# Two output projections computed as seven products of halves, with the sums of weights made on the chip

## The reference, cut to what matters

```python
mix = jnp.concatenate([y_a, y_b], axis=-1) @ w_out      # (2048 x 1024) @ (1024 x 1024), first block
x = layer_norm(alpha * x + mix, ln_g[layer], ln_b[layer])
...
y = jnp.concatenate([a, r], axis=-1) @ w_out[l]         # second block, same sizes
h = layer_norm_2(DN_ALPHA * h + y, ln_g[l], ln_b[l])
```

## Time and profile before

| | us |
|---|---|
| median of three runs | 3617.89 (3614.83 to 3624.52) |
| the profiled execution | 3618.56 |
| its span, first to last instruction | 3616.7 |

### The profile page before, as it was taken

How to read it: one execution, slowest core, us unless ns; L and a number is a source line. 1 busy time by engine, 2 the same in 40 slices (tenths; PEclk the granted TensorE clock), 3 DMA queues, 4 the chain that set the end, 5 groups by cost and what they waited for, 6 DMA issues and landing times.

```text
span 3616.7 us, 46252 instructions
## 1 busy us (share of the span) xinstructions
PE 3399.0 (94%) x17264; PEld 1815.3 (50%) x17264; DVE 1933.8 (53%) x4680; ACT 1347.7 (37%) x2565; POOL 549.5 (15%) x1001
## 2 busy tenths in 40 slices
PE   8999999999999999999989999999998898998887
PEld 3444544554455445545564455654555643455563
DVE  4326622753274337334562577816768616878742
ACT  2212211222131213123241465514775514786451
POOL 0000021002100110011120201201451111352000
PEclk9999999999999999989989999999999999998998
DMA  5230023002300210141103121021110031110011
GB/s 188 76 99 13 7 76 122 2 19 76 111 1 28 93 62 1 44 154 64 59 26 103 59 76 33 25 99 64 60 49 1 25 113 53 55 51 1 1 37 57
DMA packets 72095, 206.30 MB, mean 57 GB/s; under 512 B 6425, under 2 KB 8001, under 8 KB 71617
## 3 DMA queue, kind: packets, MB, share of 16 engines
q1 hardware_dynamic: 63536, 187.61, 15.4%
q10 hardware_dynamic: 8336, 15.74, 1.2%
HBM read 185.75 MB, written 17.58 MB: 56 GB/s over the span
## 4 chain that ended last, share of the span: by engine, by line
PE 78%; DVE 10%; ACT 6%; issue 5%; POOL 1%; DMA 1%; SPq 0%; ACTq 0%; DVEq 0%; POOLq 0%
PE bank L1989 42%; PE o_acc L2122 6%; PE bank L2105 6%; PE bank L2353 3%; PE bank L2112 3%; PE bank L2240 3%; PE bank L2272 2%; PE bank L2365 2%; PE o_acc L2379 2%; ACT prob_t L1194 1%; PE bank L2202 1%; DVE tmp L1692 1%; PE bank L2033 1%; PE bank L2039 1%; ACT index L1337 1%
## 5 line engine op out<-in xcount | busy, mean ns | idle before, releaser
L1989 PE MATMUL bank<-group_even,weights 128*128 128x512 f32 x1344 | 590.5, 597 | 11.4 <-DMA group_even<-in_x_t 5.9
L1989 PE MATMUL bank<-group_odd,weights 128*128 128x512 f32 x1344 | 591.8, 597 | 6.3 <-ACT tmp L1180 6.2
L1989 PE MATMUL bank<-y_all,weights 128*128 128x512 f32 x1024 | 441.2, 593 | 6.3 <-DVE y_all L1948 6.3
L1989 PEld LDWEIGHTS bank<-group_even,weights 128*128 128x128 f32 x1344 | 254.7, 192 | 322.6 <-issue 321.7
L1989 PEld LDWEIGHTS bank<-group_odd,weights 128*128 128x128 f32 x1344 | 254.8, 192 | 318.8 <-issue 318.3
L1139 ACT ACTIVATE probs<-probs,stat 128x512 f32<-128x512 f32 x256 | 181.7, 711 | 422.2 <-DVE stat L1456 422.2
L1989 PEld LDWEIGHTS bank<-y_all,weights 128*128 128x128 f32 x1024 | 194.2, 190 | 250.3 <-issue 243.0
L2122 PEld LDWEIGHTS o_acc<-lat,val 128*128 128x128 f32 x2048 | 238.8, 195 | 44.2 <-issue 40.2
L2122 PE MATMUL o_acc<-lat,val 128*128 128x128 f32 x2048 | 248.3, 280 | 7.7 <-DVE lat L1521 7.6
L2105 PE MATMUL bank<-k_nope,q_nope 128*32 128x512 f32 x2048 | 233.0, 595 | 0.0
L1507 DVE CUSTOM_DVE_ANT_0 probs<-bank,mask 128x512 f32<-128x512 f32 x256 | 161.4, 687 | 100.9 <-PE bank L2112 100.9
(11 more groups left out here) (396 smaller groups left out, 5151.0 us busy)
## 6 DMA issues: line engine op xcount, KB each, us to landing
weights<-in_w_in SPq DMA_DIRECT2D x101, 512.0 KB, 3.5
weights<-in_w_in_q SPq DMA_DIRECT2D x64, 512.0 KB, 3.4
weights<-in_w_out SPq DMA_DIRECT2D x64, 512.0 KB, 3.5
weights<-in_w_i SPq DMA_DIRECT2D x20, 512.0 KB, 3.4
group_odd<-in_x_t SPq DMA_DIRECT2D x8, 1024.0 KB, 9.1
group_even<-x_t SPq DMA_DIRECT2D x8, 1024.0 KB, 8.0
group_odd<-x_t SPq DMA_DIRECT2D x8, 1024.0 KB, 7.6
weights<-in_w_in_kv SPq DMA_DIRECT2D x12, 512.0 KB, 7.7
```

What stands on the lines that cost most here:

```text
L1989: ins = M(bank(*name)[:], ring[n % SLOTS][:, k * P:(k + 1) * P], rhs[:, k, :], start=(at == 0), stop=(at == chunks - 1))
```

## The change

In `1out` and `2out` the inputs are halved (chunks 0 to 3 of y, from the attention, and 4 to 7) and the 512 tokens too (EARLY and LATE, 256 each). For each pair of output chunks c, d there are seven products of 4 chunks x 256 tokens, where the two tiles of 8 chunks x 512 tokens amount to eight of that size. Four of the seven take sums of weights (t1 to t4) and four take sums of y (s1 to s4).

```diff
+OPENED_BY = {1: 1, 2: 1, 5: 5, 3: 5, 6: 6, 7: 6, 4: 6}
+def product_order(pairs):
+    out = [(0, 1)]
+    for n in range(pairs):
+        out += [(n, 6), (n, 5), (n, 7)]
+        out += [(n + 1, 1), (n, 4), (n, 2), (n, 3)] if n + 1 < pairs else [(n, 2), (n, 4), (n, 3)]
+    return out
```

```diff
+            def project_out(tag, g):
+                for at, (pair, m) in enumerate(product_order(OUT_PAIRS)):
+                    n = WSLOT[(tag + "out", g, at // 2)]
+                    if at % 2 == 0:
+                        pe.wait_ge(w_here[n % SLOTS], W_COUNT[n])
+                    if pair == 0 and m in (6, 5, 7):
+                        pe.wait_ge(y_summed, 3 * stage + {7: 1, 5: 2, 6: 3}[m])
+                    elif pair == 0 and m == 4:
+                        pe.wait_ge(made, BG * g + 2)
+                    elif pair == 0 and m == 2:
+                        pe.wait_ge(made, BG * (g + 1))
+                    elif pair == 0 and m == 3:
+                        pe.wait_ge(y_summed_late, stage + 1)
+                    claim(*name)
+                    for k in range(4):
+                        ins = M(bank(*name)[:, 0:HALF], ring[n % SLOTS][:, at % 2 * TB + k * P:at % 2 * TB + (k + 1) * P], of[:, k, :],
+                                start=(OPENED_BY[m] == m and k == 0), stop=(k == 3), skip_group_check=True)
```

```diff
+            for n, m in product_order(OUT_PAIRS):
+                if m == 1:
+                    V.scalar_tensor_tensor(out=d2, in0=d2, scalar=ALPHA, in1=got.unsqueeze(1).broadcast_to([P, 2, HALF]), ...)
+                    drains(V.scalar_tensor_tensor(out=c[:, EARLY], in0=c[:, EARLY], scalar=ALPHA, in1=got, ...), *name)
+                elif m == 2:
+                    drains(V.scalar_tensor_tensor(out=c[:, LATE], ...), *name)
+                else:
+                    to = d[:, LATE] if m in (6, 3) else d[:, EARLY] if m in (5, 7) else c[:, EARLY]
+                    drains(V.tensor_tensor(to, to, got, ALU.add), *name)
```

```diff
+            def store_pair(n):
+                act.wait_ge(pair_summed, n + 1)
+                act.dma_start(w_sums[n], pair_sums[n % 2]).then_inc(pair_stored[n % 2], 16)
+                if n + 2 < len(SUM_PAIRS):
+                    stage_pair(n + 2)
+            def store_next(g, third):
+                n = 3 * (g - 1) + third
+                if g > 0 and n < len(SUM_PAIRS):
+                    store_pair(n)
@@ ACT, first pass
                 root(("kv_sq", g), KVR, 0, (k_normed, g) if g else None)
+                if g == 0:
+                    stage_pair(0)
+                    stage_pair(1)
+                store_next(g, 0)
                 rope_tables(g)
+                store_next(g, 1)
...
                     drains(A_(val[:, BG * g + b, :], bank("v", g, b)[:], ACT.Copy), "v", g, b)
+                store_next(g, 2)
```

More of the change, by code:

```diff
@@ L409, with is_product, banks_of_tiles @@
 assert len(T) == len(TILES)
+def is_product(name):
+    return name[0] in ("1out", "2out")
+def banks_of_tiles():
+    bank, turn, used, opened = {}, {}, [0] * RING, 0
+    for name in TILES:
+        if is_product(name) and OPENED_BY[name[-1]] != name[-1]:
+            bank[name] = bank[(*name[:-1], OPENED_BY[name[-1]])]
+        else:
+            bank[name] = opened % RING
+            opened += 1
+        turn[name] = used[bank[name]]
+        used[bank[name]] += 1
+    return bank, turn
+BANK, TURN = banks_of_tiles()
 def weight_of(name):
@@ L441, in stream_of @@
 def stream_of(tiles):
-    out = []
+    out, products = [], []
     for name in tiles:
+        if is_product(name):
+            products.append((name, weights_of_product("w_out" if name[0] == "1out" else "w_out2", *name[2:])))
+            if len(products) == 2:
+                number = product_order(OUT_PAIRS).index(name[2:]) // 2
+                out.append(((*name[:2], number), None, [source for _, source in products], name))
+                products = []
+            continue
         if weight_of(name):
@@ L975, in _ @@
             pool.wait_ge(const_made, 4)
+            sum_weights()
             for g in range(G):
@@ L1982, in project @@
                 claim(*name)
-                order = list(range(chunks)) if heads_made is None else [4, 5, 6, 7, 0, 1, 2, 3]
-                for at, k in enumerate(order):
+                for k in range(chunks):
                     if parts and k % 2 == 0:
                         pe.wait_ge(x_part[k // 2], 16)
-                    if heads_made is not None and k == 0:
-                        pe.wait_ge(y1_made, heads_made)
                     ins = M(bank(*name)[:], ring[n % SLOTS][:, k * P:(k + 1) * P], rhs[:, k, :],
-                            start=(at == 0), stop=(at == chunks - 1))
+                            start=(k == 0), stop=(k == chunks - 1))
@@ L2139, in _ @@
                     wait_drained(pe, "mix", g, j)
-                for c in range(KC):
-                    project(("1out", g, c), y_of(g), KC, BG * (g + 1) if c == 0 else None)
+                project_out("1", g)
             second_begins(pe)
```

203 lines of the change are left out of this document (155 added, 48 removed).

## The result

| | median us | runs |
|---|---|---|
| kernel before | 3618.72 | 4 (3614.83 to 3624.52) |
| changed kernel | 3558.51 | 4 (3553.26 to 3564.41) |

The ratio is 0.9833 with an interval of 0.9822 to 0.9845: 60.2 us faster, where 52.4 were forecast; the time lies in the range and above its low end. Two more comparisons of the same kernels gave 59.6 and 60.5 us (ratios 0.9838 and 0.9823). The profiled execution of the changed kernel took 3564.41 us, its slowest of four, with a span of 3562.6; that is 5.9 above its own median, so its trace shows less of the gain than the medians do. One execution of a later experiment (two moves at once) ran at a mean granted clock of 0.83 and took 3970.66 us where that kernel's others took 3557.88 to 3562.68; it is left out of every comparison.

A forecast was written before the change was run, and what follows sets the result against it. PE was taken to bound the kernel. From the profiled 3618.56 us, -50.1 - 4.5 - 0.3 + 2 + 0.5 = -52.4 gave 3566.2, stated as 3566, with a range of 3550 to 3592.

The forecast's parts named there:

- PE bounds the stages, and the work falls to 7/8: Eight output projections: 224 matmuls of 256 columns replace 128 of 512, PE alone binding; -50.1 us, ends -55.0 and -28.4.
- the price of the 256-column matmul: Output projections: 0.2173 us per matmul by a straight line from 128 and 512 columns, bounds 0.2146 and 0.2294.
- Start of `2out`: Before the four `2out` stages: PE needn't wait for whole y, only the first weight slot; -4.5 us, between 0 and -6.3.
- DVE's answers: Output projections: DVE reads products before PE needs the banks; cost nothing, cover 0.7 us at start, later 1.1 a read.
- the price in the rival: Output projections: DVE answering later than 1.74 us stalls PE 64 times; 29 us at a 2.2 us answer, chance 0.04.
- Weights: Output projections: 14 slots, 3.48 us each, average need 151 GB/s, below 403; cost nothing.
- End: At the very end, the last DVE read takes 0.42 us where it was 0.69; -0.3 us.
- POOL's sums of y in the attentions: Attentions: 24 POOL sums, 1.9 us each, up to 2.6, may hold DVE; +2 us, between 0 and +22.
- First pass: First pass: weight sums on POOL with their DMA, ACT waiting for the sums; +0.5 us, range 0 to 6.
- the 98 us of room in the rival: First pass: POOL's 32 weight sums become the bound, breakeven 4.7 us a sum; +65 us at 5.1, chance 0.06.
- The first of my signs: Each projection stage starts its successor 48 to 49.5 us after its own start, 224 instructions, no idle within.
- The 1.58 us: PE's idle time before each `2out`, predicted to shrink to under 0.5 us.

The follow-up runs named there:

- two moves at once: Changed kernel with first weight-sum loads after the first rope tables and, in `2out`, x loaded behind weight slots 0 to 2: 3559.8 us, ratio 0.9830.
- the two repeats: The changed kernel run again unaltered on two chips, beside the kernel before: 3559.03 us (ratio 0.9838) and 3560.07 us (ratio 0.9823).
- the early start alone: Kernel before, with only the first tile of `2out` taking chunks 4 to 7 of y first and waiting later for the rest: 3615.25 us, ratio 0.9984.
- the second trace of the changed kernel: Profile of the unaltered changed kernel from a repeat against the kernel before; the profiled execution took 3556.62 us, the repeat's time was 3559.03 us.
- second experiment: Changed kernel with the first two pairs' weight loads issued after the first group's rope tables instead of before: 3558.95 us, ratio 0.9835.

## Why the prediction was right, and where its sizes were off

- **PE bounds the stages, and the work falls to 7/8.** Right: 224 rows without a gap, -53.1 against -50.1 forecast. The mis-sized term is the price of the 256-column matmul: 0.2173 by a straight line between the 128- and 512-column rows, 0.2158 measured, in the change and by itself. The error came from the 128-column rows: they hold about 2 ns that 256 columns don't have, which bends the line. The Trainium skill, "TensorE: Matmul & The Clock Gate", section "Wait — 56ns, not 53.3ns?", gives a fixed 2.5 ns; the measured 0.2158 is 0.2133 and 2.5 ns, and its -52.8 was the better sum: 6.60 us for each of the seven stages that end in no wait, 52.8 for eight. The same page's warning in "Back-to-back issue gap" found nothing in the trace at this width.
- **Start of `2out`.** -4.5 forecast; -5.2 in the profile (-6.1 and -5.5 in the two repeats), -4.0 in the trace by itself, where the time fell by 5.4. The limit was named rightly (the first slot behind x), and it is a matter of where DMA stands in a group: 1.04, 0, 0.07 and 0.
- **DVE's answers.** Right: cover of 1.0 us at the start, 1.2 to 1.3 later, no wait of PE. But the price in the rival was too low. It has a cost only where DVE answers later than 1.74 us, and 17 us at 2.0; one more 0.69 us a read, an answer of 1.3, already cost 10.5 us in the stages, and two, an answer of 2.0, cost 122.5 there and turned the whole change into a loss. The margin is about one DVE instruction.
- **Weights.** Nothing forecast, nothing seen: no idle time inside a stage, and a half slot of 256 KB landed in 3.4 to 3.5 us in the median.
- **End.** -0.3 forecast. It shows in PE's wait behind the last stage, 1.94 us for 2.19. The -0.75 of the table is another thing and luck of the clock: in it the 16 matmuls of one row took 9.05 us for 10.05, where 16 at the full clock take 7.03, and in the kernel before with the early start alone, whose last read is as long as ever, the stretch is 27.10 too.
- **POOL's sums of y in the attentions.** +2 forecast, nothing seen. The sums were dearer than I took (2.37 us, not 1.9) and it made no difference: of 97 DVE instructions beside them one was stretched.
- **First pass.** +0.5 forecast, +2.2 in the trace and +1.5 to +1.7 in the repeats. For its size this is the term that was furthest off. I looked for the price at ACT's waits for the sums. There the cover held: the tightest pair's sums ended at 105.76 (103.5 forecast), and ACT stored it at 108.44 with 2.7 us to spare (2.4 forecast). The price was at another place, the first sums beside DVE's chain to the first keys. And the 98 us of room in the rival, 4.7 us a sum, was wrong as a limit: at 2.6 ACT and PE already stood, for one pair.
- **What was left.** The sum of the measured terms, -56.9, is 3.3 us short of the medians' 60.2. The two profiled executions were an uneven pair, with mean granted clocks of 0.971 before and 0.968 after. Of all runs with a clock on record, those at 0.968 average 3620.8 (9 runs before) and 3561.0 (5 changed), 59.8 apart. In the second trace of the changed kernel the terms come to -58.4 of 61.9, and the 3.5 left lie between the stages; what takes them off there isn't shown.

The first of my signs was met (48.35, below 49.5), DVE's reads and ACT's rows too: ACT's at 90.19 and 105.22 came at 92.37 and 107.77, 2.2 and 2.6 us later and so within 3. The 1.58 us were under 0.5 in three of four.

## What to carry to other kernels

Where one engine is busy all through a stage and the stage is in the chain, its work can be counted in rows and the gain taken at face value; price a new shape by what two known ones have fixed, and trust the longer one, since the shortest has costs that the middle doesn't. Look at every wait that the change adds in an in-order queue by its tightest instance and by who stands behind it: average throughput put that point at 4.7 us a sum, and at 2.6 the path was already hit. Where two engines hand banks to and fro, price late answers by the waits and not by either engine's work: both then wait in turn, and here the clock fell besides, so that 6.3 us a stage by the sum of DVE's work became 15.3.

## What the runs showed of the hardware that I had not expected

- POOL's sums stretch DVE's instructions with two inputs, not only the short one of the earlier trace rows: 1.23 became 1.59 (L1630), and two of 0.70 became 1.69 each (L1610, second experiment). The Trainium skill, "GPSIMD Engine Reference", section "Key points", says that the two engines contend where DVE has two SBUF inputs; the trace agrees, and I had cited only the shared ports.
- Even so the 45.6 us of weight sums on POOL cost up to 2 us in the trace, and 24 sums of y (2.37 us each) nothing that it shows.
- At 0.2158 us a matmul a weight load of 128 columns is hidden whole; PEld is busy 42.5 of 48.3 us in such a stage.
- Half-clock stretches of PE come and go between runs of one kernel at the same place and move its time: one of 3.4 us cost 1.5 (a stretch between two stages of 294.42 for 292.94), the two rows above 2.8. A single profile can't price a term of that size.
